# Key transposes in pairs behind the probability copies, heads turned ahead of samples, state copies spread: a decoder layer on one core

## The reference

```python
proj = jnp.matmul(x_all, w_in)                       # 1024 x 3072: q, k, v of two groups of 8 heads
oa_p = moba_prompt(qa_p, ka_p, va_p, sl_a)           # causal attention inside a block of 256
oa_s = moba_sample(qa_s, ka_s, va_s, ck, cv, page_table, sl_a)   # 256 past keys from a paged cache
ob_p = dilated_prompt(qb_p, kb_p, vb_p, sl_b)
ob_s, kw_new, vw_new = dilated_sample(qb_s, kb_s, vb_s, kw, vw, sl_b)  # past keys from a state buffer
hx = layer_norm(DN_ALPHA * x_all + jnp.matmul(o_cat, w_out), ln1_g, ln1_b)
f = moe_ffn(hx, w_router, b_router, w_gate_up, b_gate_up, w_down, b_down)  # top 4 of 32 experts
hx = layer_norm(DN_ALPHA * hx + f, ln2_g, ln2_b)
```

## Time and profile before

| what | value |
|---|---|
| median of 3 runs | 1136.11 us (1134.62 to 1136.49) |
| the profiled execution: its time, its span | 1135.97 us, 1134.1 us |
| TensorE busy | 1089.8 us (96%) |
| VectorE busy | 300.2 us (26%) |
| ScalarE busy | 202.0 us (18%) |
| GpSimd busy | 33.3 us (3%) |
| moved by DMA | 454.37 MB, 401 GB/s over the span |

### The profile page before, as it was taken

One profiled execution on the slowest core, in us unless ns is written; L12 is line 12 of the kernel. 1 busy time (PEld: TensorE's weight loads), 2 busy tenths in 40 slices (PEclk: granted clock), 3 DMA queues, 4 the chain that ended last, 5 costly groups with the idle time before them and its releaser, 6 DMA issues.

```text
span 1134.1 us, 14025 instructions
## 1 busy us (share of the span) xinstructions
PE 1089.8 (96%) x5340; PEld 450.7 (40%) x5341; DVE 300.2 (26%) x734; ACT 202.0 (18%) x497; POOL 33.3 (3%) x81
## 2 busy tenths in 40 slices
PE   8999999999999999999999999999999999999996
PEld 6776654433333333333333333333333333333331
DVE  1664758430212121212121212121212021303033
ACT  1322413320202020202020202020202011111102
POOL 0111221000000000000000000000000000000001
PEclk9999999999999999999999999999999999999998
DMA  9978989999999999999999999999999999999993
GB/s 305 282 242 269 359 307 372 427 431 422 428 413 431 431 431 430 431 432 429 431 432 431 431 432 431 431 432 431 431 432 431 431 432 432 429 432 429 426 425 145
DMA packets 72484, 454.37 MB, mean 401 GB/s; under 512 B 7491, under 2 KB 36819, under 8 KB 44660
## 3 DMA queue, kind: packets, MB, share of 16 engines
q1 hardware_dynamic: 60594, 431.53, 91.7%
q10 hardware_dynamic: 10114, 11.42, 3.2%
q0 software_dynamic: 1728, 10.75, 2.6%
HBM read 450.14 MB, written 11.93 MB: 407 GB/s over the span
## 4 chain that ended last, share of the span: by engine, by line
PE 77%; DMA 15%; DVE 4%; ACT 2%; issue 1%; SPq 0%; DVEq 0%
PE bank L1160 28%; PE bank L1213 19%; DMA ring<-in_w_gate_up 15%; PE bank L1044 5%; PE bank L739 5%; PE bank L766 5%; PE bank L1240 3%; PE bank L911 2%; PE bank L769 2%; PE bank L1040 1%; PE bank L1343 1%; PE bank L870 1%; PE bank L1256 1%; ACT ybuf L1406 1%; ACT actT L1406 1%
## 5 line engine op out<-in xcount | busy, mean ns | idle before, releaser
L1160 PE MATMUL bank<-ring,xg 128*64 128x512 f32 x2032 | 445.9, 594 | 12.0 <-DMA ring<-in_w_gate_up 11.9
L1160 PEld LDWEIGHTS bank<-ring,xg 128*64 128x64 f32 x2032 | 146.8, 137 | 300.5 <-issue 298.0
L1213 PE MATMUL bank<-ring,actT 128*64 128x512 f32 x960 | 216.1, 597 | 4.2 <-ACT actT L1406 4.2
L2080 DVE TENSOR_TENSOR acc<-acc,bank 128x512 f32<-128x512 f32 x60 | 41.2, 687 | 492.5 <-PE bank L1240 492.3
L1571 ACT ACTIVATE sig<-gate 128x256 f32<-128x256 f32 x64 | 26.5, 416 | 531.5 <-DVE gate L2062 531.5
L1213 PEld LDWEIGHTS bank<-ring,actT 128*64 128x64 f32 x960 | 67.3, 137 | 120.0 <-issue 115.3
L2062 DVE TENSOR_SCALAR gate<-bank 128x256 f32<-128x256 f32 x64 | 26.8, 419 | 187.8 <-PE bank L1160 187.8
L766 PE MATMUL bank<-xT,wblk 128*128 128x288 f32 x256 | 67.4, 420 | 0.0
L1562 ACT ACTIVATE xg<-bank,small 128x128 f32<-128x128 f32 x128 | 48.1, 457 | 97.0 <-PE bank L739 96.9
L1044 PE MATMUL bank<-hx,pick 128*128 128x512 f32 x128 | 59.2, 605 | 0.0
L1406 ACT ACTIVATE ybuf<-bank 128x512 f32<-128x512 f32 x63 | 36.0, 596 | 126.6 <-PE bank L1213 87.3
(11 more groups left out here) (245 smaller groups left out, 651.7 us busy)
## 6 DMA issues: line engine op xcount, KB each, us to landing
ring<-in_w_gate_up SPq DMA_DIRECT2D x127, 2048.0 KB, 27.4
ring<-in_w_down SPq DMA_DIRECT2D x63, 2048.0 KB, 29.3
wblk<-in_w_in ACTq DMA_DIRECT2D x9, 1024.0 KB, 9.7
kring<-in_cache_k_moba SPq DMA_DIRECT2D x64, 64.0 KB, 5.1
vring<-in_cache_v_moba SPq DMA_DIRECT2D x16, 256.0 KB, 5.0
out<-in_state_k_win POOLq DMA_DIRECT2D x8, 512.0 KB, 5.8
out<-in_state_v_win POOLq DMA_DIRECT2D x8, 512.0 KB, 6.9
kring<-in_state_k_win SPq DMA_DIRECT2D x32, 128.0 KB, 5.3
```

The costliest lines, as they stand in the source:

```text
L1160: ins = nc.tensor.matmul(bank[n][64 * e:64 * e + 64, :], xg[:, k, 64 * e:64 * e + 64], w[e][:, 512 * n:512 * n + 512], start=False, stop=( ...
L1213: ins = nc.tensor.matmul(bank[4 + half][64 * e:64 * e + 64, :], actT[:, j, 64 * e:64 * e + 64], w[e][:, at:at + 512], start=(j == 0), stop ...
L2080: V.tensor_tensor(o, o, new, ALU.add).then_inc(S.added, 1)
```

## The change

Four things are moved; no arithmetic is added or removed.

1. VectorE's 16 key transposes get other slots, most in pairs, and stand in a slot behind the copy of the turned probabilities (L1838), no longer between the heads' largest values and their scaling. SP's key loads stand at the slots that follow from the table.
2. In a slot with both, TensorE turns the heads' probabilities ahead of the samples'. Of the eight slots in which heads are turned, only slot 21 has both.
3. POOL's state copies are issued in groups of 2, 2, 2, 2, 4, 4 where they were 2, 2, 4, 4, 4.
4. The mask table of the samples is loaded by a DMA of its own, issued by ScalarE in slot 4; before, one DMA before slot 0 loaded all of `att`.

```diff
-    KEY = {3: 0, 4: 1, 5: 2, 6: 3, 7: 4, 8: 5, 10: 6, 11: 7, 13: 8, 15: 9, 16: 10, 17: 11, 19: 12, 20: 13, 21: 14, 22: 15}
+    KEY = {3: (0, 1), 5: (2, 3), 7: (4, 5), 10: (6,), 11: (7,), 13: (8, 9), 14: (10,), 15: (11,), 17: (12, 13), 21: (14, 15)}
...
-            return [s for s, n in KEY.items() if n == m - KRING][0]
+            return [s for s, n in KEY.items() if m - KRING in n][0]
...
         store_v(0)
+        copy_state(2)
         store_k(1)
+        copy_state(2)
         store_k(2)
         copy_state(2)
         block_queries(1)
         pool.wait_ge(S.projected, 19)
         copy_state(4)
         pool.wait_ge(S.projected, 21)
-        copy_state(4)
-        pool.wait_ge(S.projected, 22)
         copy_state(4)
...
+            if slot in TURN:
+                head_turn(TURN[slot])
             if slot in SAMP_TURN:
                 samp_turn(SAMP_TURN[slot])
             if slot in SAMP_MIX:
                 samp_mix(SAMP_MIX[slot])
-            if slot in TURN:
-                head_turn(TURN[slot])
...
-        act.dma_start(att[:, :], att_table[:, 0:A_END]).then_inc(S.att_in, 16)
+        act.dma_start(att[:, 0:A_SAMP], att_table[:, 0:A_SAMP]).then_inc(S.att_in, 16)
...
+            if slot == 4:
+                act.dma_start(att[:, A_SAMP:A_END], att_table[:, A_SAMP:A_END]).then_inc(S.samp_table_in, 16)
...
-            if slot in KEY:
-                turn_keys(KEY[slot])
             if slot in SAMP_SCORE:
...
                 V.tensor_copy(headPT[n % 4][:, 1, :], bank[3][:, 0:384]).then_inc(S.probs_copied, 1)
+            for m in KEY.get(slot, ()):
+                turn_keys(m)
             if slot in MIX:
```

More of the change, by code:

```diff
@@ L222, in build_layer @@
         weights_ready comb_turned combT_ready bias_sums bias_added selected parted parts_ready first_slots route_ready unit0 unit1 unit2 unit3 unit4
-        unit5 unit6 unit7 unit8 unit_used first_in att_in blk_in gn_in bias_in bias_used picked gathered xtok_ready
+        unit5 unit6 unit7 unit8 unit_used first_in att_in samp_table_in blk_in gn_in bias_in bias_used picked gathered xtok_ready
         slots_turned xg_ready
@@ L1720, in samp_sum @@
         def samp_sum(q):
+            if q == 0:
+                dve.wait_ge(S.samp_table_in, 16)
             dve.wait_ge(S.samp_scored, q + 1)
```

## The result

The changed kernel took 1128.03 us, the median of four runs (1127.33 to 1128.64), beside 1135.42 for the kernel before: ratio 0.9938 [0.9927, 0.995]. Two later comparisons of the same kernel gave 0.9954 [0.9939, 0.9969] and 0.9953 [0.994, 0.9966] (E5, E13). Over all of them the median is 1129.19 of 16 executions against 1134.87 of 81 (one of them, 1613.6 us at a mean granted clock of 0.654, is left out of the ratios): 5.7 us.

The account below looks back on a forecast made before the run. The prediction took the weight stream to set the end, its start following TensorE's attention part. Terms 3.0 + 2.0 = 5.0 us, taken as 5.1: 1135.97 - 5.1 = 1130.9, plus 0.14 for the median, 1131.0; range 1128.8 to 1135.2.

Parts of the forecast that it names:

- Slots 5, 7 and 17: TensorE's waits before turning heads there: moving the key transposes ends the turning 1.0 us earlier in each, 3.0 together.
- Slot 21: TensorE's wait before turning samples: moving key 13 and turning heads first ends the turning 2.0 us earlier (1.2 to 2.4).
- The path to the end: From 654 us on, the weight stream sets the end, by when it runs without a hole and by its bytes.
- the hole: Last gap in the weight stream, at 188 to 192 us, DMA share 0.65, laid to SP's wait for key stores.
- the sum: Gain on TensorE through slots 5, 7, 17 and 21: 3.0 + 2.0 = 5.0 us (3.6 to 5.9).
- the restart: Issue of weight units 3 and 4 after the last key stores: 5.0 to 6.9 us earlier, taken as 5.1.
- the surplus: What the weight stream's restart gains beyond TensorE's own 5.0 us, at most 1.9 more; called worth little.
- The rival by which the DMA engines decide the restart: No change, chance 0.15: DMA engines, not TensorE, time the weight stream's restart; 0 to 2.2 us gained.
- The stores' landing: The last key store took 7.2 us to land; a shorter landing could bring at most 1.9 us more.
- the lock in the rule: VectorE can lock GpSimd out of its port, delaying store descriptors; then the gain is 5.0 us, not up to 6.9.
- The slower rival: Slot 18, chance 0.08: `load_v(1)`, behind key 14's load, is issued until 104.5 and lands late; 1138 to 1140 us.
- Mask table and copies at nothing: The mask table's separate load and the regrouped state copies were costed at nothing.

Follow-up runs that it names:

- E5: The changed kernel again, word for word, for more executions: 1128.89 us.
- E13: The changed kernel once more, for more executions; its profile has the slow start: 1129.52 us.
- E12: The changed kernel with the samples' turns ahead of the heads' in slot 21 again: 1131.46 us, ratio 0.9972.
- E15: The changed kernel with the samples' turns first in slot 21 and four filler products in the wait this leaves on TensorE: 1131.24 us, ratio 0.9964.
- E11: The changed kernel with ten products of zeros on TensorE ahead of the first turn: 1127.90 us, ratio 0.9951.
- E10: The kernel before with ten products of zeros ahead of the first turn and nine filler products in slot 21's wait: 1133.47 us, ratio 0.999.
- E3: The changed kernel with weight units 3 and 4 issued after one of the two store semaphores, the other waited for behind them: 1128.53 us, ratio 0.9946.
- E1: The kernel before with only the mask table's load split in two: 1134.75 us, ratio 0.9998.
- E8: The kernel before with only the key pairs and the heads' turning first, mask table and state copies as before: 1130.63 us, ratio 0.9958.
- E16: The kernel before with only the key pairs and the heads' turning first, run again: 1128.48 us, ratio 0.994.
- E14: The changed kernel with GpSimd's state copies issued as before: 1130.86 us, ratio 0.9963.
- E9: The kernel before with nine filler products on TensorE in slot 21's wait: 1134.18 us, ratio 0.9997.
- E6: The kernel before with 16 products of zeros on TensorE ahead of the first turn: 1135.02 us, ratio 0.9993.
- E4: The changed kernel with the mask table loaded in one piece, as before: 1129.44 us, ratio 0.9954.

## Why the prediction was right and where it was wrong

In slot 17 after the change, ScalarE's last sum and VectorE's next instruction:

```profile
102.99 0.19 ACT L1445 ACTIVATION_READ_ACCUMULATOR headS<-headS,small 128x1 f32 x1
```

```profile
103.21 0.17 DVE L1703 RECIPROCAL small<-small 128x2 f32<-128x2 f32 x1
```

- **Slots 5, 7 and 17** (forecast 1.0 each): 0.96, 0.97, 0.96. Right, with the reason given: the second scaling starts at 103.21, right behind ScalarE's sum at 103.18, and 0.27 of idle time is left of the 0.90. **Slot 21** (2.0, of it 1.2 for the key and 0.8 for the order): 1.83, of it 0.65 for the order by E12 and E15. Sum 4.72 where 5.0 stood; 4.70 by E13 and 4.94 by E11 against E10, each less the difference of the first scores.
- **The path to the end was wrong.** The prediction has the end set by the weight stream, "by when it starts to run without a hole". E3 closes the hole, with issues 8.5 us earlier, and gains nothing. What moved the end is when TensorE reaches the gate-and-up part: L1256 plus 928 to 931 us is the span in all 18 profiles. The gain came out near the sum all the same because the prediction put the restart at 5.1, TensorE's own 5.0, and called the surplus worth little. The rival by which the DMA engines decide the restart falls with E13, whose gain is 4.8.
- **The stores' landing.** The wait for the last stores fell from 12.2 to 10.7, so the restart gained 1.5 over TensorE's 4.7, inside the forecast's 5.0 to 6.9, and by E3 it was worth nothing. The wait is 11.3 to 12.2 in the five profiles with the old keys and 10.6 to 11.4 in those with the new, E3's apart. VectorE was as busy in the hole as before (3.68 of 4 us), so its busy time does not explain the difference. Whether the lock in the rule of the Trainium skill (SBUF — State Buffer, section "SBUF: two separate sides") has a part in the landing no run here shows.
- **The slower rival.** `load_v(1)` was issued from 95.69 to 99.57, not to 104.5, and TensorE does not wait for it in slot 18.
- **Mask table and copies at nothing**: held by E1, E8 and E16 and by the profiles; E14's executions are the open end.
- **The step that failed** is the sum: "1135.97 - 5.1 = 1130.9". It takes the profiled execution's start as the kernel's own, and the low end of the range leaves room beyond 5.1 only for the stores. That execution had the slow start, 2.3 to 2.5 us, which other executions of the same kernel don't have. And the wait of 2.42 was priced by its idle time, with nothing for the clock behind it. The forecast missed 1128.03 by 3.0: 1.2 lie in the base (1136.11 there, 1134.87 over 81), 0.6 in the gain (5.1 against 5.7 between the medians over all), and 1.2 in the four executions of the first comparison (1128.03, over 16 it is 1129.19). The last is chance, as far as the runs tell: those four took 1127.3 to 1128.6, the one profiled with the fast start and one wait for weights less; twelve more took 1127.65 to 1131.7. At equal starts the gain is 4.7 to 4.9 at L1256, near the 5.1 forecast. The rest of the 5.7 is about what the lower clock behind the removed wait is estimated at (E9), which is not shown. That the other three of the first four had the fast start too is argued from their times, not shown.

## What to carry to other kernels

Before two executions are subtracted, compare a part that the change cannot touch: here the first scores, 2.54 us apart, were almost a third of the 8.6 between the two profiles. Price a wait of TensorE by when the next work ends, since the clock can fall behind it, as in E6 and E4; and state a range with the spread of the executions in it, not only the unknown costs. Units freed earlier were worth nothing here as long as the loads behind them still waited for the engine that frees their buffers, so count the gain where that engine arrives. And before calling a hole in a stream the limit, close it by itself, as E3 does.

## What the runs showed of the hardware

- TensorE's start differs from execution to execution: products at 684 to 820 ns until some 13 us, or at 406, with a granted clock that reads 1.00 either way. Of the 14 profiles without products of zeros ahead of the first turn eight were fast and six slow; all four with them were fast. The Trainium skill (TensorE: Matmul & The Clock Gate, section "What's actually happening") says that the number of slow products varies between runs of a kernel, and the traces agree; it puts the cost under 1% of a typical span, and here it is 2.3 of 1130, yet two fifths of the gain. Whether these products are slow for the page's reason the granted clock, at 1.00, does not show.
- Behind a wait of 2.42 us the granted clock fell to 0.50 in two of three profiles and cost 1.57; behind one of 2.31 us it was 0.67 over the next 4 us (E4); behind one of 1.24 it stayed at 1.00 (E12, one profile).
- Closing a hole in the weight stream moved 422 GB/s instead of 250 from 180 to 190 us and 306 instead of 397 from 210 to 220 (E3 against E13), and the time did not change.
